# Differential attention: VectorE rotates the two kinds of sparse keys two and three steps later, and splits the second weight half one step earlier

## What is computed

```python
def _token_mix(h, w_in, ...):
    z = h @ w_in
    (gu, gv, dq, dk, dv, nq, nkc, nvc, nks, nvs, nkw, nvw, ng) = jnp.split(z, pts, axis=-1)
    y_a = _gmlp_sgu(gu, gv, ...)                 # gv, gu
    y_b = _diff_attention(dq, dk, dv, lam, ...)  # 4 heads, 2 score maps each, over 512 positions
    y_c = _nsa(nq, nkc, nvc, nks, nvs, nkw, nvw, ng, ...)
    return jnp.concatenate([y_a, y_b, y_c], axis=-1) @ w_out

def _diff_attention(q, k, v, lam, ...):
    ...
        p = _masked_softmax(s, t[:, None] >= pos[None, :])
        a = p[:, :, 0] - lam * p[:, :, 1]
        return jnp.einsum('bhqk,bhkd->bhqd', a, v)

def _nsa(...):
    q = _rope(q, pos)
    k_slc = _rope(kv(ks), pos)   # selected blocks
    k_win = _rope(kv(kw), pos)   # window
```

## Time and profile before

| | |
|---|---|
| median of 3 runs | 2620.91 us |
| lowest and highest | 2620.72, 2622.26 us |
| the profiled execution, its own time | 2622.49 us |
| its span | 2621.2 us |
| mean granted TensorE clock | 0.997 of full |
| busy, PE, DVE, ACT | 2593.9, 1562.8, 1041.1 us |
| mixer l = 0, the place of the change | 1068 to 1106 us |
| mixer l = 1, the same | 2072 to 2109 us |

### The profile page before, as it was taken

One profiled execution on the slowest core, in us unless ns is written; L12 is line 12 of the kernel. 1 busy time (PEld: TensorE's weight loads), 2 busy tenths in 40 slices (PEclk: granted clock), 3 DMA queues, 4 the chain that ended last, 5 costly groups with the idle time before them and its releaser, 6 DMA issues.

```text
span 2621.2 us, 33927 instructions
## 1 busy us (share of the span) xinstructions
PE 2593.9 (99%) x13989; PEld 2153.6 (82%) x13989; DVE 1562.8 (60%) x2777; ACT 1041.1 (40%) x1803; POOL 15.0 (1%) x43
## 2 busy tenths in 40 slices
PE   7999999999999999999999999999999999999999
PEld 5788888898888898777888889888889776988888
DVE  7766555358666466787766637753346787633334
ACT  4652343444222245665322224322235665422223
POOL 1000000000000000000000000000000000000000
PEclk9999999999999999999999999999999999999999
DMA  8255433225555233412655524532333511323222
GB/s 263 81 177 173 129 113 106 80 96 177 194 192 194 91 122 109 121 33 65 210 198 190 172 85 157 193 129 97 97 101 117 145 33 49 97 97 97 97 93 69
DMA packets 298241, 330.15 MB, mean 126 GB/s; under 512 B 13410, under 2 KB 248678, under 8 KB 298088
## 3 DMA queue, kind: packets, MB, share of 16 engines
q1 hardware_dynamic: 297716, 327.44, 38.8%
q10 hardware_dynamic: 372, 0.55, 0.1%
HBM read 319.56 MB, written 2.10 MB: 123 GB/s over the span
## 4 chain that ended last, share of the span: by engine, by line
PE 95%; DVE 3%; ACT 1%; DMA 0%; SPq 0%; issue 0%; DVEq 0%
PE bank L546 27%; PE bank L548 27%; PE bank L547 27%; PE bank L600 3%; PE bank L2577 2%; PE bank L2604 2%; PE bank L2211 1%; PE bank L574 1%; PE bank L575 1%; PE bank L576 1%; DVE w_lo L514 1%; DMA mw<-in_w_mod 0%; PE bank L907 0%; PE bank L2387 0%; DVE x L794 0%; PE bank L590 0%
## 5 line engine op out<-in xcount | busy, mean ns | idle before, releaser
L546 PE MATMUL bank<-h_lo,w_hi 128*128 128x512 f32 (+1 forms) x2496 | 938.4, 376 | 0.6 <-DVE h_lo L745 0.6
L548 PE MATMUL bank<-h_hi,w_lo 128*128 128x512 f32 (+1 forms) x2496 | 920.3, 369 | 0.0
L547 PE MATMUL bank<-h_hi,w_hi 128*128 128x512 f32 (+1 forms) x2496 | 919.1, 368 | 0.0
L514 DVE TENSOR_TENSOR w_lo<-raw,w_hi 128x1024 fp32r<-128x1024 f32 (+1 forms) x420 | 489.5, 1201 | 366.8 <-ACT w_hi L508 366.6
L508 ACT ACTIVATE w_hi<-raw 128x1024 fp32r<-128x1024 f32 (+1 forms) x420 | 420.3, 1036 | 351.2 <-PE bank L548 336.6
L546 PEld LDWEIGHTS bank<-h_lo,w_hi 128*128 128x128 f32 x2496 | 471.9, 189 | 81.8 <-issue 4.4
L547 PEld LDWEIGHTS bank<-h_hi,w_hi 128*128 128x128 f32 x2496 | 472.3, 189 | 78.5 <-issue 4.1
L548 PEld LDWEIGHTS bank<-h_hi,w_lo 128*128 128x128 f32 x2496 | 471.1, 189 | 78.2
L546 PE MATMUL bank<-a_lo,w_hi 128*128 128x512 f32 (+1 forms) x1056 | 389.0, 368 | 0.0
L548 PE MATMUL bank<-a_hi,w_lo 128*128 128x512 f32 (+1 forms) x1056 | 384.7, 364 | 0.0
L547 PE MATMUL bank<-a_hi,w_hi 128*128 128x512 f32 (+1 forms) x1056 | 384.3, 364 | 0.0
(11 more groups left out here) (354 smaller groups left out, 2283.8 us busy)
## 6 DMA issues: line engine op xcount, KB each, us to landing
swf<-in_w_ada SPq DMA_DIRECT2D x60, 1024.0 KB, 7.6
raw<-in_ffn_w_gate SPq DMA_DIRECT2D x44, 1024.0 KB, 5.3
raw<-in_ffn_w_up SPq DMA_DIRECT2D x44, 1024.0 KB, 5.3
raw<-in_w_in SPq DMA_DIRECT2D x40, 1024.0 KB, 5.1
raw<-in_ffn_w_down SPq DMA_DIRECT2D x32, 1024.0 KB, 4.9
raw<-in_w_in SPq DMA_DIRECT2D x32, 512.0 KB, 5.2
raw<-in_ffn_w_down SPq DMA_DIRECT2D x16, 768.0 KB, 4.2
mw<-in_w_mod SPq DMA_DIRECT2D x8, 1024.0 KB, 11.7
```

Source lines behind the costliest of these rows:

```text
L514: nc.vector.tensor_tensor(o, r, half(w_his[place_of[i]], i, h)[0].bitcast(F32), ALU.subtract).then_inc(*w_lo.up((i, h)))
L546: nc.tensor.matmul(o, w1, al, start=start, stop=False)
L547: nc.tensor.matmul(o, w1, ah, start=False, stop=False)
L548: return nc.tensor.matmul(o, w2, ah, start=False, stop=stop)
```

## The change

In VectorE's program of the mixer three calls are put in another order among the attention's steps. The number of steps up to dve_vv is seven before and after (13 to 19). Before: 13, rotation 8, second weight half of vv, 14, rotation 9, 15 to 19. After: 13, second weight half, 14, 15, rotation 8, 16, 17, rotation 9, 18, 19. No other engine's program is touched.

```diff
         dve_hidden_silu(l, 0)
         dve_w(("kk", l), 2, 0)
         steps(1)
+        dve_w(("kk", l), 2)
+        steps(2)
         dve_rope(l, 8)
-        dve_w(("kk", l), 2)
-        steps(1)
+        steps(2)
         dve_rope(l, 9)
-        steps(5)
+        steps(2)
         dve_vv(l)
         dve_kc(l)
         dve_w(("vv", l), 2)
```

## The result

The changed kernel takes 2629.91 us (median of 7 runs, 2626.96 to 2631.09), the kernel before 2620.91 us (7 runs, 2620.16 to 2623.17). The ratio is 1.0031, 95% interval 1.0022 to 1.004: slower by 9.0 us, 0.3%. The profiled execution took 2631.09 us, its span is 2629.5 us, 8.3 us more than before.

The account below looks back on a forecast made before the run. TensorE, busy 99% of the span, was taken as the bound. Delays from gv's late load, 3.05 us in the first mixer and 3.4 in the second, add 6.4 to 2620.91: 2627.3 us, range 2621.5 to 2630.0.

Parts of the forecast that it names:

- Part 1: ks's rotation moved behind item 15: TensorE's waits of 0.65 and 0.25 us go, -0.9 us in each mixer.
- Rival (d): Item 15's banks were held by an engine other than VectorE, so the edit does nothing there; no chance given.
- Part 2, the queue: kw's rotation behind step 17 ends 7.7 us later; SyncE waits for it, so gv's load goes out at 1088.7.
- The landing: gv's load takes 6.0 and 6.4 us in the two mixers, making ScalarE late by 3.25 and 3.6 us.
- Rival (a): gv lands like lone loads, 5.0 and 5.2 us: 2625.2 us; 0.25 together with landings between, down to the skill's.
- rival (c): gv's and gu's loads share the DMA queues, gv lands in about 8 us: 2631 us; chance 0.05.
- The chain to item 1's scores: gv's lateness passes through ScalarE and VectorE to TensorE at NSA item 1: 3.05 and 3.4 us.
- The sum: Both mixers' delays together, +6.4 us on the median 2620.91: 2627.3 us, 0.24% slower; chance as summed 0.60.
- the forecast's own range: The narrower range given for the forecast as summed, 2626.0 to 2627.9 us.
- Rival (b): The wait for item 14's banks goes and gv is still in time: 1.8 us faster, 2619.1 us; chance 0.10.

Follow-up runs that it names:

- e7: The changed kernel with gv's raw load still behind kw's copies but issued ahead of the small gm_w_s and gm_b_s loads; 2628.23 us, ratio 1.0029 to before.
- e6: The kernel before with only gv's raw load issued ahead of the copies of ks and kw on SyncE; 2621.40 us, ratio 1.0003 to before.
- e1: The changed kernel with gv's raw load issued ahead of the copies of ks and kw on SyncE; 2619.10 us, ratio 0.9992 to before.
- e2: The changed kernel with kw's rotation one step earlier, ahead of step 17 instead of behind it; 2619.96 us, ratio 0.9997 to before.
- e4: The changed kernel with compressed-score matmuls repeated on TensorE, half ahead of gv and all ahead of NSA item 1; 2627.50 us, ratio 1.0023 to before.
- e9: The changed kernel with compressed-score matmuls repeated on TensorE ahead of NSA item 1 only; 2628.17 us, ratio 1.0027 to before.
- e3: The kernel before with one more SyncE wait, holding kw's copies until VectorE has copied vv's first half out; 2627.81 us, ratio 1.0025 to before.
- e10: The changed kernel with half of the compressed-score matmuls repeated on TensorE ahead of gv only; 2629.34 us, ratio 1.0031 to before.

## Why the prediction was right

Forecast 2627.3 us in 2621.5 to 2630.0, slower; measured 2629.91. By its steps:

- *Part 1.* Less the 0.35 us of the start, item 14's first reduction came at 1074.6 and TensorE's scores of item 15 at 1076.2, as forecast. One wait more than forecast lies ahead of them: the combination of item 12 stood 0.66 us for ScalarE, which ended just as TensorE's scores did and cost nothing. Both waits of the earlier trace rows went, as summed, and ks's rotation cost nothing. Rival (d) falls with that.
- *Part 2, the queue.* kw's rotation was to end at 1086.4 and ended at 1086.44, gv's load was to go out at 1088.7 and went at 1088.73. Some of this closeness is luck: the profile was shifted by 0.35 us, and a_lo held VectorE for 0.6 us (to the rotation's start at 1084.43) and not 0.8. (Before, four GpSimd instructions ran beside it, from 1084.36; after, they ran at 1090.50. The longer a_lo fits what e7 shows of such overlaps, but wasn't tested by itself.)
- *The landing.* 6.0 and 6.4 us taken, 6.1 and 6.8 measured. The estimate by the Trainium skill's fit for the GpSimd path (DMA: Bandwidth & Descriptors, Anatomy of one DMA), 4.4 us, was off by 1.7 and 2.4: no landing of gv's load in these kernels was under 5.5 us. What the load has ahead of it on the queues counts: in e6, issued right behind another 1 MB load, it took 8.1 us, in e1 9.8. Rival (a), the short landing, falls with that, and rival (c), with its 8 us, too: gu's load, 0.4 us behind gv's, left its landing at 6.1 and 6.8 us.
- *The chain to item 1's scores.* 3.05 and 3.4 us taken, 2.84 and 3.5 measured. TensorE's two waits were forecast as 1.5 us at gv and some 2 us at item 1: 1.4 and 2.2.
- *The sum* was 6.4 us. These terms measured 2.84 + 3.54 = 6.38. That it comes so close is in part luck: one mixer was 0.2 us under its term, the other 0.1 us over.
- *What was missing* is the last 1.57 us in the first mixer. "From there all engines stand to one another as before, shifted" took it that a wait of TensorE costs its own length. This one cost 1.57 us more, because TensorE came out of it to a granted 1.2 GHz for 3.4 us. In the second mixer the lower clock fell between gv's wait and item 1's, where TensorE had to wait for VectorE anyway: the wait at item 1 shrank to 0.9 us, and the clock cost nothing. I gave no chance to such a term, though the trace of the kernel before has a case of it: the 1.9 us wait at 610 us with 6.8 us at 1.2 GHz behind it. Alone it takes the forecast to 2628.9, out of the forecast's own range; with the start and the scatter of the runs the time came within 0.1 us of the full range's upper end, 2630.0. That it stayed inside is luck: the interval of the ratio reaches 2631.4 us.
- *Rival (b)*, the gain kept, is what e1 and e2 do. Its deciding point, kw's rotation done by 1083.0, before a_lo, was the right one: e2 crosses it by one step.
- The medians differ by 9.0 us and the spans by 8.3. 0.35 of the 8.3 are the start's, as shown above, and no effect of the edit. The other 0.7 us are how the two profiled executions lie in the scatter of their kernels' runs.

No version beats the kernel before by more than its interval leaves open. The one that keeps the change's order and issues gv's load first is ahead by 1.7 us by its stages.

## What to carry to other kernels

Before moving work down an in-order engine, list who waits for its result and what stands behind that waiter in *its* order: here the moved rotation's result was first read 24 us after it was made, but a load that had nothing to do with it and only came later in SyncE's program had 4.3 us. Here that load, started ahead of the waits for results, took the whole loss away (e1). Where a chain of other engines meets TensorE without slack, a delay passes in full, and a TensorE wait of 2 us may cost more than its length.

## What the runs showed of the hardware that I had not expected

- A TensorE wait of 2.0 to 2.2 us in a kernel that is otherwise 99% busy was followed, in six cases of eight, by 3.4 us at a granted 1.2 GHz, at a price of 1.6 us where TensorE was the one waited for. The kernel before has such a place too: behind the wait of 1.9 us at about 610 us, eleven of the twelve profiles show 3.4 or 6.8 us at 1.2 GHz, and e2's, with the same wait, none. The Trainium skill, TensorE: Matmul & The Clock Gate, Part 1, makes the clock depend on how busy TensorE has been of late. The traces agree in kind: the filled kernels e4 and e9 kept 2.4 GHz in both mixers. They don't say why equal waits had both outcomes.
- GpSimd and VectorE slow each other: four GpSimd products went from 1.73 to 3.67 us and two VectorE splits from 2.36 to 2.79 us where they overlapped (e7; the spans of GpSimd are rough). The Trainium skill, SBUF — State Buffer, Who interferes with whom, says that a VectorE instruction with two SBUF inputs contends with a GpSimd one that reads SBUF. Both are of that kind, and the trace agrees.
- The same 1 MB load behind the same issues landed in 6.1 to 6.9 us in the change, e3, e4, e9 and e10, a scatter nearly as large as part 1's gain in a mixer.
